# Output rows of a decoder layer's cross-attention: the contraction taken in two halves, outermost, with four open sums

## The reference

```python
o = jnp.einsum('bhsm,bmhd->bshd', p.astype(v.dtype), v).reshape(B, S, D)
h = h + o @ w_xo
xn = rmsnorm(h, g_moe_norm)
logits = (xn @ w_router + b_router)
top_v, top_e = lax.top_k(logits, 4)
gate = softmax(top_v)
g, u = split(xn[rows of expert e] @ w_gate_up[e] + b_gate_up[e])
g, u = min(g, 7), clip(u, -7, 7)
y[rows of e] += gate * (((u + 1) * g * sigmoid(1.702 * g)) @ w_down[e] + b_down[e])
```

## Time and profile before

| what | value |
|---|---|
| median of 3 runs | 1186.83 us |
| lowest, highest | 1186.59, 1187.05 us |
| the profiled execution | 1186.32 us |
| its span in the trace | 1184.6 us |
| granted TensorE clock, mean | 0.998 of full speed |
| TensorE matmuls busy | 1117.3 us (94%) |
| VectorE, ACT, GpSimd busy | 319.4, 233.0, 36.4 us |
| moved by the transfers | 445.50 MB, mean 376 GB/s |

### The profile page before, as it was taken

The page is one execution under the profiler, slowest core; times in us unless marked ns, Lnnn a source line. Parts: engine busy times, 40 slices in busy tenths (PEclk is TensorE's granted clock), DMA queues, the critical chain, the costliest instruction groups (busy, mean ns, idle before and its releaser), DMA issues.

```text
span 1184.6 us, 12853 instructions
## 1 busy us (share of the span) xinstructions
PE 1117.3 (94%) x5466; PEld 497.6 (42%) x5467; DVE 319.4 (27%) x719; ACT 233.0 (20%) x460; POOL 36.4 (3%) x35
## 2 busy tenths in 40 slices
PE   8999999999999999999999999999999999999896
PEld 7887678753333333333333333333333333333332
DVE  5787665233111111222111111111111111111112
ACT  6575665341100000110010000000000000000002
POOL 0000240220000000000000000000000000000000
PEclk9999999999999999999999999999999999999999
DMA  9915337769999999999999999999999999999995
GB/s 362 351 49 183 103 143 273 264 267 426 427 429 427 427 428 427 429 426 428 426 428 429 427 429 427 428 427 428 427 427 429 427 428 428 427 429 426 428 428 224
DMA packets 44586, 445.50 MB, mean 376 GB/s; under 512 B 6096, under 2 KB 10288, under 8 KB 19728
## 3 DMA queue, kind: packets, MB, share of 16 engines
q1 hardware_dynamic: 42784, 444.38, 90.1%
q10 hardware_dynamic: 1744, 0.28, 0.1%
HBM read 443.60 MB, written 1.05 MB: 375 GB/s over the span
## 4 chain that ended last, share of the span: by engine, by line
PE 59%; DMA 35%; DVE 3%; ACT 2%; issue 1%; POOL 0%; DVEq 0%; ACTq 0%; POOLq 0%
PE ps L2074 19%; DMA R<-in_w_gate_up 16%; PE ps L2083 11%; DMA MK<-in_w_gate_up 4%; DMA R<-in_w_down 4%; PE ps L1570 4%; DMA XMT<-in_w_gate_up 4%; DMA A<-in_w_gate_up 4%; PE ps L2103 4%; DMA XM<-in_w_gate_up 4%; PE ps L2050 3%; PE ps L1590 3%; PE ps L1592 3%; PE ps L1591 3%; PE ps L1934 2%; PE ps L1826 2%
## 5 line engine op out<-in xcount | busy, mean ns | idle before, releaser
L2074 PE MATMUL ps<-R,convT 128*64 128x512 f32 x1104 | 246.5, 594 | 17.4 <-DMA R<-in_w_gate_up 17.4
L1471 DVE TENSOR_SCALAR A<-ps 128x512 f32<-128x512 f32 x30 | 20.7, 692 | 644.2 <-PE ps L2074 644.2
L2074 PEld LDWEIGHTS ps<-R,convT 128*64 128x64 f32 x1104 | 76.6, 137 | 173.8 <-issue 135.5
L2083 PE MATMUL ps<-R,A 128*64 128x512 f32 x592 | 131.9, 593 | 1.5 <-DMA R<-in_w_down 1.5
L943 ACT ACTIVATE A<-A 128x512 f32<-128x512 f32 x30 | 18.9, 630 | 470.0 <-DVE A L1471 470.0
L2083 PEld LDWEIGHTS ps<-R,A 128*64 128x64 f32 x592 | 41.5, 137 | 79.0 <-issue 75.1
L2103 PE MATMUL ps<-A,convT 64*128 64x512 f32 x248 | 61.6, 615 | 1.4 <-ACT A L950 0.7
L950 ACT COPY A<-ps 128x512 f32<-128x512 f32 x30 | 17.6, 585 | 221.3 <-PE ps L2083 221.3
L2050 PE MATMUL ps<-H,convT 128*64 128x512 f32 x256 | 60.4, 592 | 0.0
L2074 PE MATMUL ps<-XMT,convT 128*64 128x512 f32 x208 | 47.0, 594 | 2.8 <-DMA XMT<-in_w_gate_up 2.8
L2065 PE MATMUL ps<-A,convT 96*64 96x512 bf16 x192 | 32.5, 388 | 15.4 <-ACT A L948 13.7
(11 more groups left out here) (323 smaller groups left out, 1288.7 us busy)
## 6 DMA issues: line engine op xcount, KB each, us to landing
R<-in_w_gate_up SPq DMA_DIRECT2D x69, 2048.0 KB, 44.7
R<-in_w_down SPq DMA_DIRECT2D x37, 2048.0 KB, 47.1
XMT<-in_w_gate_up SPq DMA_DIRECT2D x13, 2048.0 KB, 45.7
QK<-in_w_gate_up SPq DMA_DIRECT2D x12, 2048.0 KB, 47.2
MK<-in_w_gate_up SPq DMA_DIRECT2D x12, 2048.0 KB, 47.7
A<-in_w_gate_up SPq DMA_DIRECT2D x11, 2048.0 KB, 42.3
XM<-in_w_gate_up SPq DMA_DIRECT2D x11, 2048.0 KB, 46.1
XM<-in_w_down SPq DMA_DIRECT2D x6, 2048.0 KB, 37.8
```

The costliest lines, as they stand in the source:

```text
L2074: last = mm(bank(b)[s * SLOTS:(s + 1) * SLOTS, :], xg[:, 4 * (j % 2) + 2 * c + j // 2, :], w[:, c * 2 * FF + at + s * BANK:c * 2 * FF + at ...
L2083: last = mm(bank(o)[s * SLOTS:(s + 1) * SLOTS, :], h[:, c, i * SLOTS:(i + 1) * SLOTS], w[:, c * D + s * BANK:c * D + (s + 1) * BANK], star ...
```

## The change

`w_o2` is now laid out by chunks: place 6 holds chunks 0 to 3 with all 1024 columns, place 8 chunks 4 to 7, and each of the two loads brings one such half of the rows of w_xo. TensorE does chunks 0 to 3 of all four sums first, and raises `pe_xo` to 1 after them; then chunks 4 to 7 of each, which close the sums and raise `pe_xo` to 2, 3, 4 and 5. SP waits for 1 before fill 6 and for 5 before fill 8. The transposes of H's second tile and the routers are placed anew, three matmuls of `keep_warm` go, and VectorE's `top_four(0)` stands behind the second half of tile 1's rows.

```diff
--- before.py
+++ after.py
@@ -108,7 +108,7 @@
         w_cnv = R[:, 10240:10240 + KC * 3 * CONVW].rearrange("p (k n) -> p k n", k=KC)
         w_out = R[:, 0:8192].rearrange("p (k n) -> p k n", k=KC)
         w_xv = R[:, 0:8192].rearrange("p (k n) -> p k n", k=KC)
-        w_o2 = R[:, 16384:24576].rearrange("p (h k n) -> p h k n", h=2, k=KC)
+        w_o2 = R[:, 16384:24576].rearrange("p (k n) -> p k n", k=KC)
         tail = R[:, 16384:24576]
         w_a = A[:, :].rearrange("p (k n) -> p k n", k=KC)
         w_c1 = A[:, :].rearrange("p (v m n) -> p v m n", v=2, m=MC)
@@ -484,8 +484,8 @@
                 sp.dma_start(w_a, chunked(w_xq[0])).then_inc(ld_q2, 16)
                 sp.wait_ge(pe_ss, 2)
                 sp.wait_ge(pe_mo, 2 * T)
-                for n in range(2):
-                    sp.dma_start(w_o2[:, n], chunked(w_xo[0, :, n * BANK:(n + 1) * BANK])).then_inc(ld_o2, 16)
+                for h in range(2):
+                    sp.dma_start(w_o2[:, 4 * h:4 * h + 4, :], chunked(w_xo[0, h * BANK:(h + 1) * BANK, :])).then_inc(ld_o2, 16)
 
                 def fill(e, j, slot):
 
@@ -519,11 +519,11 @@
                     if n == 5:
                         sp.wait_ge(pe_two, TWO["oT", 1])
                     if n == 6:
-                        sp.wait_ge(pe_xo, 3)
+                        sp.wait_ge(pe_xo, 1)
                     if n == 7:
                         sp.wait_ge(act_part, 3)
                     if n == 8:
-                        sp.wait_ge(pe_xo, 4)
+                        sp.wait_ge(pe_xo, 5)
                     if n == 9:
                         sp.wait_ge(pe_lg, T)
                     if n == 10:
@@ -1383,7 +1383,7 @@
                 pv_first(1)
                 first("oT", 1, 4, first_half(oT2, 1))
                 def token_rows(t, n):
-                    dve.wait_ge(pe_xo, 2 * t + n + 1)
+                    dve.wait_ge(pe_xo, 2 * t + n + 2)
                     hn = H[:, t, n * BANK:(n + 1) * BANK]
                     link(V.tensor_tensor(hn, hn, bank(4 * t + 2 + n), ALU.add), dve_h2)
 
@@ -1407,11 +1407,11 @@
                 reciprocal_root(0, 1)
                 token_rows(1, 0)
                 gain_rows("h2T", 1, R_MOE, 0)
+                token_rows(1, 1)
+                gain_rows("h2T", 1, R_MOE, 1)
                 dve.wait_ge(pool_moe, 9)
                 dve.wait_ge(ld_misc, 64)
                 top_four(0)
-                token_rows(1, 1)
-                gain_rows("h2T", 1, R_MOE, 1)
                 reciprocal_root(1, 1)
                 top_four(1)
 
@@ -1935,7 +1935,7 @@
                     return last
 
                 def wo(c, n):
-                    return w_o2[:, n, c, :]
+                    return w_o2[:, c, n * BANK:(n + 1) * BANK]
 
                 def ot(t):
                     return lambda c: oT2[:, t, c, :]
@@ -1990,12 +1990,16 @@
                 pv2(1)
                 pe.wait_ge(ld_o2, 32)
                 ready("oT", 0)
-                half_rows(0, 0, ot(0), wo).then_inc(pe_xo, 1)
+                half_rows(0, 0, ot(0), wo, range(4))
                 ready("pv", 1)
                 eight_transposes("oT", 1, XS[:, 1, :])
-                half_rows(0, 1, ot(0), wo).then_inc(pe_xo, 1)
+                half_rows(0, 1, ot(0), wo, range(4))
                 ready("oT", 1)
-                half_rows(1, 0, ot(1), wo).then_inc(pe_xo, 1)
+                half_rows(1, 0, ot(1), wo, range(4))
+                half_rows(1, 1, ot(1), wo, range(4)).then_inc(pe_xo, 1)
+                half_rows(0, 0, ot(0), wo, range(4, KC)).then_inc(pe_xo, 1)
+                half_rows(0, 1, ot(0), wo, range(4, KC)).then_inc(pe_xo, 1)
+                half_rows(1, 0, ot(1), wo, range(4, KC)).then_inc(pe_xo, 1)
                 pe.wait_ge(dve_h2, 2)
                 eight_transposes("h2T", 0, H[:, 0, :])
 
@@ -2010,12 +2014,11 @@
                         last = tr(bank(4 + n)[:, (c % 4) * P:(c % 4 + 1) * P], src[:, c * P:(c + 1) * P])
                     last.then_inc(pe_two, 1)
 
-                half_rows(1, 1, ot(1), wo, range(4))
+                half_rows(1, 1, ot(1), wo, range(4, KC)).then_inc(pe_xo, 1)
                 pe.wait_ge(dve_h2, 3)
                 four_transposes(0, H[:, 1, :])
                 ready("h2T", 0)
-                router(0, range(KC)).then_inc(pe_lg, 1)
-                half_rows(1, 1, ot(1), wo, range(4, KC)).then_inc(pe_xo, 1)
+                router(0, range(4))
 
                 def y_start(t):
 
@@ -2023,11 +2026,11 @@
                         mm(bank(Y_BANK + 2 * t + n), ident[:], H[:, t, n * BANK:(n + 1) * BANK], start=True, stop=False,
                            skip_group_check=True)
 
+                pe.wait_ge(dve_h2, 4)
+                four_transposes(1, H[:, 1, :])
+                router(0, range(4, KC)).then_inc(pe_lg, 1)
                 pe.wait_ge(dve_two, EVICT["h2T", 1])
                 router(1, range(4))
-                pe.wait_ge(dve_h2, 4)
-                four_transposes(1, H[:, 1, :])
-                keep_warm(3)
                 pe.wait_ge(dve_two, EVICT["h2T", 2])
                 router(1, range(4, KC)).then_inc(pe_lg, 1)
                 y_start(0)
```

## The result

The changed kernel took 1188.04 us in the median of 16 runs, the kernel before 1187.09 beside it. The ratio is 1.0016, with a 95% interval of 1.0009 to 1.0022: slower by about 0.16%, where I had said 0.8 us faster. (The ratios here weigh all executions and can differ from that of the two medians, which is 1.0008; the means are 1188.82 and 1186.99.) The median lies inside the 0.2% that I called "within", but on the other side and just outside my range. One of the 16 executions, at a mean clock of 0.847, took 1304.97 and is not in the ratio.

What follows compares the result with a forecast made beforehand. The end was taken to be set by when the stream of 192 expert weight fills becomes continuous. Fill 11's 0.8 us off the profiled 1186.32 gave 1185.5; with the median 0.5 above, 1186.0, range 1184.5 to 1188.0.

Steps and rivals of the forecast that it cites:

- within: Whole kernel: the time stays within about 0.2%, 2.4 us, which a measurement of this kernel can tell; chance 0.80.
- The timing of the stage: Stage before the experts: fills 5, 6, 7 and 8 issued 3.4, 6.9, 4.2 and 2.2 us earlier, expert 0 0.2 earlier.
- the new idle: TensorE, before the last transposes: a new wait of about 0.6 us, ending at about 260.2.
- tile 1's ranking: VectorE, before expert 0: it starts at 263.9 instead of 264.10, right behind tile 0's ranking.
- fill 11's dependence on expert 0: SP's queue: fill 11 waits for expert 0's matmuls, not the output rows, so it goes at 275.15 instead of 275.35.
- the ranking in series: VectorE: tile 0's ranking, free before, is now on the path and eats what the earlier logits gave.
- The sum: Start of the expert stream: fill 11's gain, bounded between 0.1 and 1.7 us, taken as 0.8 us for the kernel.
- rival (c): TensorE before expert 0: the clock falls from 2.4 to 1.2 GHz; over 1189.2, the whole about 1197; chance 0.05.
- the line that costed the removed warming matmuls at nothing: TensorE, stage before the experts: three warming matmuls go that lay in a wait; no time charged for it.
- Rival (a): Expert stream: a fill issued near its forerunner's end loses nothing, or expert 0 starts earlier; 1184.4 us; chance 0.12.
- my optimistic end: Expert stream: fill 11 lands like a lone fill, 7.7 us after issue, at 282.85 instead of 284.55, 1.7 earlier.
- My reading of fill 6: SP's queue: fill 6 goes 6.9 us earlier, but early fills only bring the hole forward; fill 11's issue sets the rest.

Runs made afterwards that it cites:

- b_rank: The kernel before with tile 0's ranking behind the second half of tile 1's rows on VectorE, TensorE's order old: 1188.27 us against 1187.28, ratio 1.0014.
- a_wide: The changed kernel with one unused matmul of 512 columns in the idle ahead of the last transposes: 1185.81 us against 1187.14 for the kernel before, ratio 0.9991.
- a_wide_2: The changed kernel with one unused 512-column matmul in the idle ahead of the last transposes, repeated on another chip: 1186.68 us against 1187.38 for the kernel before, 0.9995.
- b_nowarm: The kernel before without its three warming matmuls, nothing else: 1189.08 us against 1187.28, ratio 1.0011.
- a_sums_late6: The changed kernel with half the start of the sums between the routers and fill 6 held until the third sum closed: 1186.42 us against 1187.14 for the kernel before.
- h_tail: The changed kernel's halves with the old tail: router 0 inside the last half row, ranking before the last sum, warming matmuls back: 1189.32 us against 1187.28, ratio 1.0017.
- a_sums: The changed kernel with half the start of the sums between the routers, tile 0's router whole before the last transposes: 1186.39 us against 1187.14 for the kernel before.
- a_warm2: The changed kernel with two warming matmuls of 128 columns in the new idle: 1186.51 us against 1187.28 for the kernel before, ratio 0.9995.

## Why the prediction was wrong

**The timing of the stage: right.** Fills 5 to 8, the new idle (0.64 for "about 0.6"), tile 1's ranking (265.24, less 1.25 is 263.99, for 263.9) and fill 11's dependence on expert 0 came out as worked. b_rank shows the price of the ranking in series by itself: fill 11 goes 0.8 later.

**The sum: right where the clock holds.** I took 0.8 us; a_wide's profile shows 1.0 from the half rows on, and the medians of a_wide_2 and a_wide 0.7 and 1.3. At 300 us a_wide had 371.86 MB still to move, 0.9 us less than the kernel before. The executions with a mean clock of 0.999 or more say the same: those of a_wide and a_wide_2 took 1185.0 to 1186.0 (five), those of the kernel before 1185.7 to 1187.2 (fourteen, median 1186.2). The changed kernel had none in 27.

**The step that failed is rival (c), and the line that costed the removed warming matmuls at nothing.** I gave the fall of the clock 0.05, said that "it decides at an idle longer than the kernel has shown", and set against it an idle of 0.85 us at 219.84. That was the wrong row: behind that idle stand matmuls of 256 columns, and ahead of it too, but for 1.1 us of transposes. The fall came at a shorter idle, of 0.64 us, after some 5 us of transposes and matmuls of 32 columns; and b_nowarm suggests that the three matmuls were not free. Whether the narrow work, the idle or both let it fall is not shown. For the width: the clock fell in all three profiles with the tail as changed or with narrow matmuls in the idle, and in none of the three with a wide one there. Against it as the whole cause: the falls at 266 (a_sums_late6) and 1160 (h_tail), right behind waits and close behind wide matmuls. I also mis-sized the price: (c) took 12 us of work at half speed and got 1197. The rows show a fall of 3.4 us (264.2 to 267.6), which put fill 11 1.3 late. A small price with a high chance stood in my text as a large price with a small one. With 1.3 at an even chance the forecast would have been about 1186.7, no change. The six executions above 1189.8 may have paid more.

**A second thing was not in the sum at all**: the fall at 138 us. It is worth about 1 us in an execution (0.95 of the 1.25 offset in the profile after; 0.3 was there already), and it belongs to both kernels: it stood in three of the eleven profiles that have no matmul added there. That the changed kernel has it more often is not shown; in its two profiles it stood both times. Nor is it all that shifts the start: in a_sums the half rows began 1.06 late without it, as its first matmul of 512 columns began at 10.08 instead of 8.97.

**Rival (a)** (fill 11 loses nothing at the joint) is not borne out. Fill 11 did land 7.7 after its issue in the changed kernel, my optimistic end, but because it was issued 1.3 late, when the line was empty; in a_wide, issued within 0.2 of the forecast, it took 8.7. **My reading of fill 6** was right: a_sums_late6. What I missed about the joints is h_tail: when fills 8 to 11 each find nearly empty engines, some rate is lost at each joint, 0.8 us in all against a_warm2.

What stays open: how often the clock falls at each place in unprofiled executions, of which only the mean is known; what lets it fall, as said above, and how much of that is chance of timing (P), which no run here rules out; why the changed kernel was 0.16% slower in its first runs and 0.04% on the later chip (the intervals overlap; six of 15 executions had mean clocks of 0.994 or less there, one of 11 here); and whether a narrow matmul helps at all, since a_warm2 and a_wide ran on different chips.

The Trainium skill ("TensorE: Matmul & The Clock Gate", Why this matters for your kernels) asks for no long idle gaps between bursts of matmuls. By it this order was safe, for its longest gap here was 0.64 us. The traces of the changed kernel differ: the clock fell with no gap over 0.64 us, TensorE otherwise busy with narrow matmuls.

## What to carry to other kernels

When an order is changed, read not only where each engine waits, but how wide TensorE's work is between the waits: a wide piece that stood among routers, transposes or one-column sums may be what held the clock, and to take a warming matmul out of a wait may have a price (1.1 us by the means in b_nowarm). If such a piece must move, put another there, best one that has to be done anyway (a_sums), else an unused one in the wait that the new order opens (a_wide). Then look at the clock in more than one trace: a_sums kept it up, a_sums_late6 with the same order on TensorE did not. And find the one transfer whose issue sets the stream before moving the others: here seven microseconds on fill 6 were worth nothing, while 0.8 on fill 11 was worth 0.7.

## What the runs showed of the hardware that I had not expected

- The granted clock fell to 0.50 for 3.4 us at a time, at 138, 263 to 266, 1140 and 1160 us, in executions whose mean was 0.995 to 0.998. It came back by itself while TensorE worked on.
- With equal issues of fills 10 to 15, fill 15 landed 2.3 us later when fills 8 and 9 had gone 2.5 and 1.5 us later (h_tail and a_warm2). The stream as a whole was only 0.36 MB, 0.8 us, behind.
